# Expert gate and up weights in transfers of 8 MB with 64 KB rows, and a router chain by token tiles

## Chip, cores and metric

The kernel runs on one core of one Trainium2 chip. The metric is the device time of one execution in microseconds. The median of three executions of the kernel before is 1241.34 us (1241.11 to 1243.54).

## What is computed

One decoder layer and a final norm, for one sequence of 256 tokens of width 1024, all in float32:

```
h = x + hybrid_mixer(rms_norm(x))            # gated linear attention beside dilated window attention
h = h + memory_cross_attention(rms_norm(h))  # 4 heads into 256 memory tokens
f = rms_norm(h)
logits = f @ w_router + b_router             # 32 experts
top_logit, top_e = top_k(logits, 4); gate = softmax(top_logit)
h = h + sum over the 4 experts e of gate * ( swiglu(f @ w_gate[e] + b_gate[e], f @ w_up[e] + b_up[e]) @ w_down[e] + b_down[e] )
out = rms_norm(h)
```

`swiglu` is clamped. Every expert is worked through, with up to 64 of its tokens at a time; further rounds follow only if an expert got more than 64.

## The kernel before

The program is written by hand, engine by engine, with semaphores; nothing is reordered by a scheduler. Each of the five engine blocks (`sp`, `pool`, `act`, `dve`, `pe`) runs its own list.

**Dense part.** The mixer's and the cross-attention's weights arrive as 1 MB halves (`HALVES`, `w_dense`) in three raw buffers. ScalarE cuts each half into a float16 high part (line 643) and VectorE into a low part (L969, and for the first half in two pieces, `ahead_cut`, L1020); TensorE multiplies high by high, high by low and low by high (`PASSES`). `feature_major` and `token_major` are the two loops. At the start VectorE and ScalarE square one tile of x each, the normed x is transposed, and `high_T` and `low_T` make its two parts. The results of TensorE go through eight PSUM banks whose use is set by the list `FILLS`: `fill` takes the bank of a name, `take` waits until it is full, `emptied` until it is free again.

**Router.** The output projection of the cross-attention has four blocks, `xo{n}{t}`: column half n, token tile t (128 tokens). VectorE adds each to h (L1289), ScalarE squares it (L657), TensorE transposes h (`residual_T`, L1748), and ScalarE or VectorE copies the transposes to `fT` with the gain `g3` (`routed_T`). After the last block the mean squares of both tiles become roots on GpSimd (`root(6, 8)`, L568), h is split into high and low parts (L890, L1297), the logits of both tiles are scaled (L1313), the top four are found, a matrix product with a triangle gives each token its place (L1789), and two comparisons (L1352) make the selection matrices that the experts' gather needs.

**Experts.** 32 experts in 8 groups of 4 (`EG`), `body` once per group: group 0 written out, 1 to 3 and 4 to 6 in loops, group 7 written out with pieces. Per expert j there are six units of 2 MB, in the order of `ORDER`: gate and up of the first half of the hidden columns, gate and up of the second half, down first half, down second half. Unit v of a group is v = 6j + i. Units go through a ring of `NSLOT` = 8 slots; unit v uses slot `home_index(v)` = (v + 2) mod 8. `unit_left(v - 8)` makes the sync queue wait until TensorE has used up the unit that was in the slot: gate and up units are released by `h_full` at the end of a gate/up pass (L1888), down units by `dn_used` and `y_full` (L1910). The sync queue's loop in groups 1 to 6 is

```
for v in range(0, per, 2):
    unit_left(v - NSLOT, k * EG, z)
    unit_left(v + 1 - NSLOT, k * EG, z)
    load_pair(v, n * EG + v // UPE, z)      # 4 MB: 128 partitions x 32 KB
```

On TensorE an expert is: gate/up pass of the first half (32 matmuls of 512 columns, L1888), transposes (L1901), pass of the second half, transposes, down (32 matmuls, L1910). At expert 0 of a group two gathers (L1829) stand before the first pass and two inside it, after 8 matmuls; the scatter of the expert before (L1839) stands before the group's gathers or between the passes. In group 0 units 10 to 15 are loaded in pieces as the first expert frees its slots (`reused`, `gu_used`). In group 7 the last experts' units come in pieces (`LAST_PIECES`).

**End.** VectorE multiplies the sums by the final gain (`gained`, L1419), ScalarE squares them (L936), VectorE asks for the root (`asked`, L1426), GpSimd takes it, ScalarE and VectorE scale one half each (L940, L1437), and four stores follow.

## Time and profile before

| | |
|---|---|
| median of three executions | 1241.34 us |
| the profiled execution | 1242.41 us |
| its span | 1240.7 us |
| TensorE busy | 1153.2 us (93%), 6687 matmuls |
| VectorE, ScalarE, GpSimd busy | 411.6, 261.6, 20.9 us |
| mean granted TensorE clock | 0.986 |
| moved by the DMA engines | 458.38 MB, 369 GB/s over the span |
| sync queue's share of 16 DMA engines | 87.8% |
| chain that ended last | TensorE 61%, DMA 29%, sync queue 3%, ScalarE 2%, VectorE 2% |

The profiled execution lies 1.07 us above the median. "Busy" counts an engine's instructions, not its waits. The page cuts the span into 40 slices of 31 us: the DMA engines' share is 35 to 85% in the first 11 slices, and 90% or more from the 14th to the last but one, where they move 418 to 435 GB/s. The chain that ended last is followed back from the end, at each step to whatever released it. "DMA ring<-in_w_down" in it is the time from a transfer's issue to its landing.

### The profile page before, as it was taken

To read this page: it belongs to the slowest core of one execution; us is meant where nothing else is said; L and a number is where in the kernel's file an instruction comes from. 1 tells how busy PE (TensorE), PEld (TensorE's weight loads), DVE (VectorE), ACT (ScalarE), POOL (GpSimd) and SP (SyncE) were. 2 spreads that over 40 slices of the span, in tenths; PEclk is the share of its full clock that TensorE was granted. 3 is DMA by queue.
4 is the path that set the end of the run, shared out by engine and by line. 5 is a ranking of instruction groups with operands and counts; after the bars stand their busy time and mean duration, and the time that the engine had idled before them with its cause. 6 is when DMAs were issued, how large, how long until landed. Compare 5 with 4: busy or idle time off the path is not lost.

```text
span 1240.7 us, 16139 instructions
## 1 busy us (share of the span) xinstructions
PE 1153.2 (93%) x6687; PEld 576.8 (46%) x6687; DVE 411.6 (33%) x803; ACT 261.6 (21%) x450; POOL 20.9 (2%) x40
## 2 busy tenths in 40 slices
PE   8999999999999999999989887998998898889887
PEld 7888989887433333333323232432332233224322
DVE  6789474665422222222122112211221122122112
ACT  5655464464400010010001000100110010001001
POOL 4000000000000000000000000000000000000000
PEclk9999999999899999999999999999999999999999
DMA  8455524986699999999999999999999999999996
GB/s 329 173 204 183 190 76 182 382 316 244 239 420 395 430 418 434 429 435 428 435 427 435 430 433 429 431 429 432 431 431 433 431 431 431 435 428 435 419 419 264
DMA packets 30117, 458.38 MB, mean 369 GB/s; under 512 B 3584, under 2 KB 3600, under 8 KB 8816
## 3 DMA queue, kind: packets, MB, share of 16 engines
q1 hardware_dynamic: 28800, 454.57, 87.8%
q0 software_dynamic: 832, 2.51, 0.6%
q8 instruction: 39, 0.64, 0.2%
q10 hardware_dynamic: 432, 0.55, 0.1%
q14 instruction: 14, 0.11, 0.0%
HBM read 456.57 MB, written 1.05 MB: 369 GB/s over the span
## 4 chain that ended last, share of the span: by engine, by line
PE 61%; DMA 29%; SPq 3%; issue 2%; ACT 2%; DVE 2%; POOL 0%; DVEq 0%; ACTq 0%; POOLq 0%
PE bank L1888 22%; DMA ring<-in_w_down 16%; DMA ring<-in_w_gate_up 12%; PE bank L1910 10%; PE bank L1495 4%; PE bank L1472 4%; PE sums L1553 3%; PE sums L1472 3%; SPq L431 3%; PE sums L1839 3%; PE sums L1495 2%; PE bank L1829 2%; PE bank L1553 2%; PE bank L1901 2%; DMA ring<-in_w_dense 1%
## 5 line engine op out<-in xcount | busy, mean ns | idle before, releaser
L1888 PE MATMUL bank<-ring,reg_a 128*64 128x512 f32 x2016 | 457.9, 606 | 42.5 <-DMA ring<-in_w_gate_up 41.8
L1888 PEld LDWEIGHTS bank<-ring,reg_a 128*64 128x64 f32 x2016 | 142.4, 139 | 324.4 <-issue 263.4
L1910 PE MATMUL bank<-ring,reg_ol 128*64 128x512 f32 x1024 | 227.0, 595 | 14.5 <-DMA ring<-in_w_down 12.8
L1389 DVE TENSOR_TENSOR masks<-bank,bT 128x256 f32<-128x256 f32 x64 | 27.2, 424 | 449.7 <-PE bank L1901 449.7
L1910 PEld LDWEIGHTS bank<-ring,reg_ol 128*64 128x64 f32 x1024 | 79.2, 137 | 141.1 <-issue 133.8
L625 ACT ACTIVATE reg_t<-bank 128x512 f32<-128x512 f32 x64 | 38.2, 597 | 440.5 <-PE bank L1888 240.5
L969 DVE SCALAR_TENSOR_TENSOR ring<-ring 128x2048 f16<-128x2048 f32 x47 | 107.3, 2289 | 40.1 <-ACT ring L643 39.8
L643 ACT ACTIVATE ring<-ring 128x2048 f16<-128x2048 f32 x47 | 89.5, 1910 | 32.7 <-PE sums L1553 14.1
L926 ACT ACTIVATE masks<-masks 128x256 f32<-128x256 f32 x64 | 26.7, 417 | 326.4 <-DVE masks L1390 326.4
L1839 PE MATMUL sums<-reg_t,reg_g 64*128 64x512 f32 x256 | 70.1, 634 | 5.5 <-ACT reg_t L625 5.5
L1376 DVE COPY reg_t<-bank 128x512 f32<-128x512 f32 x32 | 22.1, 691 | 159.2 <-PE bank L1888 159.2
L1901 PEld LDWEIGHTS bank<-ident,reg_t 128*128 128x128 f32 x256 | 26.8, 140 | 42.7 <-DVE reg_t L1376 21.8
L1839 PEld LDWEIGHTS sums<-reg_t,reg_g 64*128 64x128 f32 x256 | 20.0, 185 | 55.3 <-issue 42.7
L1901 PE MATMUL bank<-ident,reg_t 128*128 128x128 f32 x256 | 42.0, 287 | 2.5 <-DVE reg_t L1376 1.7
L1553 PE MATMUL sums<-reg_a,ring 128*128 128x256 f16 x384 | 42.3, 273 | 0.0
L1829 PE MATMUL bank<-reg_t,reg_m 128*128 128x256 f16 x256 | 34.0, 291 | 6.5 <-issue 5.8
L1553 PEld LDWEIGHTS sums<-reg_a,ring 128*128 128x128 f16 x384 | 37.5, 98 | 4.6 <-issue 0.3
L1369 DVE TENSOR_TENSOR reg_a<-bank,g 128x512 f32<-128x512 f32 x16 | 11.1, 692 | 80.3 <-PE bank L1829 80.3
L1472 PE MATMUL bank<-reg_a,ring 128*128 128x256 f16 x336 | 37.5, 273 | 0.0
L1829 PEld LDWEIGHTS bank<-reg_t,reg_m 128*128 128x128 f16 x256 | 25.2, 104 | 22.7 <-issue 18.7
L1472 PEld LDWEIGHTS bank<-reg_a,ring 128*128 128x128 f16 x336 | 32.9, 98 | 3.8
L1472 PE MATMUL sums<-reg_a,ring 128*128 128x256 f16 x240 | 27.3, 273 | 1.8 <-DVE reg_a L976 1.8
(323 smaller groups left out, 884.8 us busy)
## 6 DMA issues: line engine op xcount, KB each, us to landing
ring<-in_w_gate_up SPq DMA_DIRECT2D x52, 4096.0 KB, 29.8
ring<-in_w_down SPq DMA_DIRECT2D x26, 4096.0 KB, 30.8
ring<-in_w_dense SPq DMA_DIRECT2D x47, 1024.0 KB, 5.1
ring<-in_w_gate_up SPq DMA_DIRECT2D x10, 2048.0 KB, 9.6
ring<-in_w_gate_up SPq DMA_DIRECT2D x16, 1024.0 KB, 25.5
ring<-in_w_down SPq DMA_DIRECT2D x6, 2048.0 KB, 11.0
ring<-in_w_gate_up SPq DMA_DIRECT2D x16, 512.0 KB, 14.2
ring<-in_w_down SPq DMA_DIRECT2D x12, 512.0 KB, 7.2
```

The lines of the kernel that those rows point to most:

```text
L431: sp.dma_start(home[:, o:o + n], src.rearrange("e p n -> p (e n)")).then_inc(done, 16)
L625: return act.activation(dst, src, ACT.Copy)
L643: act.activation(cut[u % EARLY][:, 0, :], raw[u % EARLY], ACT.Copy, scale=WS).then_inc(w_high, 1)
L969: dve.scalar_tensor_tensor(cut[u % EARLY][:, 1, :], raw[u % EARLY], WS, cut[u % EARLY][:, 0, :], ALU.mult, ALU.subtract).then_inc(w_low, 1)
L1472: ins = mm(b[:, i * T:(i + 1) * T], w[:, pw, c, o:o + P], rhs[:, px, c, :], start=(c == 0 and k == 0), stop=(c == nk - 1 and k == 2))
L1495: ins = mm(b[:, i * n:(i + 1) * n], lhs[:, px, c, t * P:(t + 1) * P], w[:, pw, c, 0:n], start=(c == 0 and k == 0), stop=(c == nk - 1 and k ...
L1553: ins = mm(b[:, i * T:(i + 1) * T], w[:, pw, i, c, :], aT[:, px, c, :], start=(c == 0 and k == 0), stop=(c == C - 1 and k == 2))
L1829: ins = mm(pt[2 + q % 2][:, i * T:(i + 1) * T], f16[:, part, t, 2 * q + i, :], sel[:, t, :], start=(t == 0 and part == 0), stop=(t == TT - ...
L1839: ins = mm(acc[t][nh][:], selT[rows_h, j, t, :], y[rows_h, :], start=False, stop=last and j == EG - 1)
L1888: ins = mm(pt[nh][col:col + 64, :], xg[:, c, j * SLOTS:(j + 1) * SLOTS], loaded(v + i, C, c), start=(c == 0), stop=(c == C - 1))
L1901: ins = pe.transpose(pt[i][:, c * P:(c + 1) * P], hs[:, 4 * i + c, :], ident[:])
L1910: ins = mm(pt[2][64 * nh:64 * nh + 64, :], actT[:, 4 * i + c, :], w[:, nh * 512:(nh + 1) * 512], start=(i == 0 and c == 0), stop=(i == 1 a ...
```

## The change

**8 MB transfers.** `WHOLE` holds the first units of those experts whose four gate and up units lie in four neighbouring slots: v = 0, 6 and 18, that is experts 0, 1 and 3 of a group. In groups 1 to 6 the four units are loaded by two transfers, of partitions 0 to 63 and 64 to 127, each with rows of 64 KB. Both wait for the release of unit v + 3 - 8. TensorE waits for both before it begins the expert.

```diff
+        WHOLE = [UPE * j for j in range(EG) if home_index(UPE * j, None) + 4 <= NSLOT]
...
                 for v in range(0, per - UPE if last else per, 2):
+                    if not last and v in WHOLE:
+                        o = home_index(v, z) * WIDE
+                        whole = A["w_gate_up"][bass.ds(n * EG + v // UPE, 1)]
+                        for half in range(2):
+                            unit_left(v + 3 - NSLOT, k * EG, z)
+                            rows = slice(64 * half, 64 * half + 64)
+                            sp.dma_start(ring[rows, o:o + 4 * WIDE], whole[:, rows].rearrange("e p n -> p (e n)"))\
+                                .then_inc(home_of(v + 2 * half, z, False)[1], 16)
+                        continue
+                    if not last and v - 2 in WHOLE:
+                        continue
...
                         if z is first_round and not first and pieces == 1:
+                            u = v - v % UPE
+                            if not last and v == u and u in WHOLE:
+                                _, other, c2 = home_of(u + 2, z, first)
+                                pe.wait_ge(other, k * (16 * per // NSLOT) + c2)
                             _, done, count = home_of(v - v % 2, z, first)
```

The last expert's first pair is loaded in 4 pieces each in place of 2, and three semaphores are used twice.

The sync queue's loop over a group, before, from v = 0 (a row with `waits` and no DMA is the wait of the DMA under it; `a_h_full` is the release by a gate/up pass, `a_y_full,a_dn_used` that by the down passes):

```order
L422 ISA [waits a_y_full,a_dn_used]
L422 DMA ring<-in_w_gate_up 128x8192
L438 ISA
L422 ISA [waits a_h_full]
L422 DMA ring<-in_w_gate_up 128x8192
L422 ISA [waits a_h_full]
L422 DMA ring<-in_w_down 128x8192
L422 ISA [waits a_y_full,a_dn_used]
L422 DMA ring<-in_w_gate_up 128x8192
```

The same place in the changed program:

```order
L535 ISA [waits a_h_full]
L535 DMA ring<-in_w_gate_up 64x16384
L535 ISA [waits a_h_full]
L535 DMA ring<-in_w_gate_up 64x16384
L429 ISA [waits a_h_full]
L429 DMA ring<-in_w_down 128x8192
L445 REGISTER_ALU
L535 ISA [waits a_h_full]
L535 DMA ring<-in_w_gate_up 64x16384
L535 ISA [waits a_h_full]
L535 DMA ring<-in_w_gate_up 64x16384
```

Experts 0 and 1 now have two 64x16384 transfers each (16384 elements of 4 bytes per row) behind one and the same release of gate/up units; the down pairs and expert 2's pairs stand as before.

**Router by tiles.** The blocks come in the order xo00, xo10, xo01, xo11. The gain `g3` is multiplied into the router weights instead of into the transposed h. Square, root, logits, choice, place and selection are made for tile 0 while TensorE is at xo11, and for tile 1 after it. VectorE's new list (ScalarE's and TensorE's follow it; `ROUTING` sets their banks):

```diff
+            dve.tensor_tensor(w_rt[:], w_rt[:], bc(g3[:], E), ALU.mult).then_inc(consts, 1)
...
+            residual(0, 0)
+            residual(0, 1)
+            mean_square(0)
+            dve.memset(ranked[:, :, 0:TOPK], -FAR)
+            residual(1, 0)
+            routed_T("0b", 4, 4)
+            f_low_part(0, 0)
+            f_low_part(1, 0)
+            chosen(0)
+            residual(1, 1)
+            placed(0)
+            routed_T("1c", 4, 2)
+            mean_square(1)
+            routed_T("1d", 6, 2)
+            emptied(dve, "pos0")
+            selected(0, 0)
+            chosen(1)
+            f_low_part(0, 1)
+            placed(1)
...
+            def awake(n):
+
+                emptied(pe, "rl1")
+                for _ in range(n):
+                    mm(pt[BANK["rl1"]][:], f16[:, 0, 0, 0, :], wide, start=True, stop=True)
```

`awake(2)` stands twice on TensorE: before and after the products that give the places of tile 1 and the totals. It writes to a bank that nobody reads.

TensorE before, from the third output block (bank) to the places:

```order
L1495 MATMUL bank<-ring,reg_t 128x512 x12
L1748 MATMUL bank<-ident,h 128x128 x8
L1495 MATMUL bank<-ring,reg_t 128x512 x12
L1766 MATMUL bank<-reg_a,w_rt 32x256 x4
L1748 MATMUL bank<-ident,h 128x128 x8
L1773 MATMUL bank<-fold,reg_t 128x32 x2
L1778 MATMUL bank<-w_rt,reg_a 128x32 x8
L1785 MATMUL sums<-reg_m 128x512 x4
L1789 MATMUL bank<-route,tri_s 128x64
```

TensorE now, the same stretch:

```order
L1550 MATMUL bank<-ring,reg_t 128x512 x12
L1831 MATMUL bank<-ident,h 128x128 x8
L1550 MATMUL bank<-ring,reg_t 128x512 x6
L1846 MATMUL bank<-reg_a,w_rt 32x128 x8
L1831 MATMUL bank<-ident,h 128x128 x4
L1550 MATMUL bank<-ring,reg_t 128x512 x3
L1837 MATMUL bank<-fold,reg_t 128x32
L1550 MATMUL bank<-ring,reg_t 128x512 x3
L1846 MATMUL bank<-reg_a,w_rt 32x128 x4
L1869 MATMUL bank<-route,tri_s 128x32
L1831 MATMUL bank<-ident,h 128x128 x4
L1876 MATMUL bank<-w_rt,reg_a 128x32 x4
```

The router's matmuls of tile 0 (128 columns), four transposes and the fold now stand inside the last output block, in place of the 256-column ones behind it.

VectorE before, from h's first low part to the selection (`reg_ol` holds the logits and the top eight, `route` the choice and the places, `reg_t` the selection, `reg_m` h's low part):

```order
L1297 SCALAR_TENSOR_TENSOR reg_m<-h,st,reg_m 128x512
L1313 SCALAR_TENSOR_TENSOR reg_ol<-bank,st,b_rt 128x32 x2
L1318 MAX reg_ol<-reg_ol 128x8 x2
L1320 TENSOR_SCALAR st<-reg_ol 128x2
L1321 MEMSET reg_ol 128x2x4
L1323 MATCH_REPLACE reg_ol<-reg_ol 128x36 x2
L1325 TENSOR_TENSOR route<-reg_ol 128x64
L1297 SCALAR_TENSOR_TENSOR reg_m<-h,st,reg_m 128x512
L1328 SCALAR_TENSOR_TENSOR route<-bank,route 128x64
L1330 MEMSET st 128x1
L1331 MEMSET st 128x1
L1352 TENSOR_TENSOR reg_t<-route,iota_s 128x256 x2
```

VectorE now, from tile 1's choice to its selection:

```order
L1347 SCALAR_TENSOR_TENSOR reg_ol<-bank,st,b_rt 128x32
L1350 MAX reg_ol<-reg_ol 128x8
L1351 TENSOR_SCALAR st<-reg_ol 128x1
L1352 MEMSET reg_ol 128x4
L1353 MATCH_REPLACE reg_ol<-reg_ol 128x36
L1354 TENSOR_TENSOR route<-reg_ol 128x32
L1340 SCALAR_TENSOR_TENSOR reg_m<-h,st,reg_m 128x512
L1361 SCALAR_TENSOR_TENSOR route<-bank,route 128x32
L1389 MEMSET st 128x1
L1366 TENSOR_TENSOR reg_t<-route,iota_s 128x256
```

One tile's operations stand where two tiles' stood, and h's low part comes after the choice.

**Start.** The second tile of x is loaded by ScalarE's queue. q_g is multiplied with the highs of all chunks first, then with x's lows, then with the weight's lows, its two halves in two banks (`q_g`, `q_g1`); k_g likewise. VectorE makes all of x's low parts before the second half of the first weight's.

```diff
+            def highs_first(outs, w, cols, before):
+
+                for k, (pw, px) in enumerate(PASSES):
+                    for c in range(C):
+                        before(k, c)
+                        for b, o in zip(outs, cols):
+                            ins = mm(b, w[:, pw, c, o:o + P], aT[:, px, c, :], start=(k == 0 and c == 0),
+                                     stop=(k == 2 and c == C - 1))
...
-            for q in range(2):
+            for q in range(4):
                 low_T("x_T", q, aT, vT[:, 0:8])
             ahead_cut(AHEAD, HALF, w_high, 1, w_low)
-            for q in range(2, 4):
-                low_T("x_T", q, aT, vT[:, 0:8])
```

**End.** In the last group the scatter of expert 30 stands whole before expert 31's gate pass. ScalarE's square of tile 0 no longer waits for VectorE's gain product, and VectorE makes tile 1's product first:

```diff
-            for t in range(TT):
-                dve.wait_ge(acc_full, 2 * t + 1)
-                gained(t, 0)
-            for t in range(TT):
-                asked(t)
+            dve.wait_ge(acc_full, 3)
+            gained(1, 0)
+            asked(0)
+            gained(0, 0)
+            asked(1)
```

## Rows read from the trace of the kernel before

**Rows 1.** Windows: stretch, busy us (count) per engine, TensorE clock, DMA share, GB/s

```profile
250.00:300.00 50.00, 49.37 (x424) 43.52 (x423) 30.93 (x43) 29.83 (x57) 0.70 (x1) 1.00 0.66 250
...
340.00:360.00 20.00, 19.79 (x96) 7.25 (x94) 3.80 (x9) 1.27 (x3) 0.00 (x0) 1.00 1.02 411
...
900.00:1000.00 100.00, 89.14 (x405) 30.81 (x405) 22.96 (x57) 7.18 (x15) 0.00 (x0) 0.98 1.00 431
```

**Rows 2.** Sync queue's waits, whole program: total us, times, longest

```profile
SPq L438 <- PE bank L1888: 483.4, 53, 20.5
```

**Rows 3.** TensorE in order of time, group 1: start, us, line, what, [idle before]

```profile
427.58 2.74 PE L1910 MATMUL bank<-ring,reg_ol 128*64 128x512 f32 x12
...
432.94 1.92 PE L1829 MATMUL bank<-reg_t,reg_m 128*128 128x256 f16 x16
435.01 1.94 PE L1888 MATMUL bank<-ring,reg_a 128*64 128x512 f32 x8
...
438.73 5.37 PE L1888 MATMUL bank<-ring,reg_a 128*64 128x512 f32 x24
...
461.05 7.07 PE L1888 MATMUL bank<-ring,reg_a 128*64 128x512 f32 x32
...
485.27 7.04 PE L1888 MATMUL bank<-ring,reg_a 128*64 128x512 f32 x32
```

**Rows 4.** TensorE in order of time, group 4

```profile
916.97 7.09 PE L1888 MATMUL bank<-ring,reg_a 128*64 128x512 f32 x32 [0.75 <-DMA ring<-in_w_gate_up]
...
926.69 7.09 PE L1888 MATMUL bank<-ring,reg_a 128*64 128x512 f32 x32 [0.98 <-DMA ring<-in_w_gate_up]
...
946.13 8.78 PE L1888 MATMUL bank<-ring,reg_a 128*64 128x512 f32 x32 [2.64 <-DMA ring<-in_w_gate_up]
```

**Rows 5.** Group 0's last two issues, line 431, 393 to 395 us

```profile
L431 SPq DMA_DIRECT2D ring<-in_w_down x2: 328/380/431, 393.7 to 394.1; - x2
...
DMA to landing us min/median/max: 10.0/12.2/14.5
```

**Rows 6.** Sync queue in order of time, group 1's second and fourth gate pair

```profile
413.23 0.34 SPq L422 DMA_DIRECT2D ring<-in_w_gate_up  x1
...
444.33 0.33 SPq L422 DMA_DIRECT2D ring<-in_w_gate_up  x1
```

**Rows 7.** DMA issues with KB and median us to landing; last, line 431 at 315.0

```profile
h<-in_w_gate_up SPq DMA_DIRECT2D x1, 1024.0 KB, 4.7
...
out<-reg_m ACTq DMA_DIRECT2D x2, 256.0 KB, 2.5
...
DMA to landing us min/median/max: 8.3/8.3/8.3
```

**Rows 8.** Windows of 2 us at the first gather and in group 4

```profile
322.00:324.00 2.00, 1.23 (x7) 0.87 (x7) 2.00 (x5) 1.39 (x4) 0.24 (x1) 0.50 0.02 8
...
947.00:949.00 2.00, 2.00 (x6) 0.48 (x4) 0.00 (x0) 0.00 (x0) 0.00 (x0) 0.50 0.95 410
```

**Rows 9.** Window in which 8 KB rows are loaded

```profile
1180.00:1200.00 20.00, 19.40 (x92) 6.61 (x90) 5.08 (x13) 1.43 (x3) 0.00 (x0) 1.00 1.01 422
```

**Rows 10.** Chain of waits from the last output block to the first expert

```profile
316.90 0.71 POOL st L568
...
318.47 0.75 DVE reg_m L1297
...
322.82 3.57 PE bank L1829 x16
326.39 3.06 PE bank L1888 x8
```

**Rows 11.** TensorE in order of time, start

```profile
14.92 9.47 PE L1472 MATMUL sums<-reg_a,ring 128*128 128x256 f16 x84 [1.09 <-DVE reg_a L976]
...
42.14 5.41 PE L1495 MATMUL bank<-ring,reg_a 128*128 128x256 f16 x48 [1.15 <-DVE ring L969]
```

**Rows 12.** All engines in order of time, end

```profile
1233.40 1.02 ACT L936 ACTIVATE reg_g<-sums 128x1024 f32<-128x1024 f32 x1 [2.07 <-PE sums L1839]
```

312 lines of the change are left out of this document (178 added, 134 removed).

## Prediction

> **What bounds the kernel now.** I read the windows by stage first. Up to 300 us the DMA engines move 250 GB/s while TensorE is busy 49.4 of 50 us; from 340 us on they are busy all the time, at 430 GB/s and more, and between 900 and 1000 us TensorE is busy for 89 of 100 us [rows 1]. So the experts' half of the program is bound by the transfers, and TensorE fills in behind them. The sync queue's waits say what the transfers wait for: a ring slot that the gate and up matmuls free, 53 times, 483 us in all [rows 2]. It costs nothing today, as long as enough is queued when the slot comes free.
>
> TensorE's order of time gives the pace of both. In group 1 it isn't held up: expert 1 takes 485.27 - 461.05 = 24.2 us. Expert 0 takes 26.0 us from its first gate matmul (435.01), and 4.7 us of scatter and gather lie between the end of the last down matmuls before it (430.3) and that matmul [rows 3]. A group is 4 x 24.2 + 1.8 + 4.7 = 103.3 us of TensorE. In group 4 its waits end on landings 9.72 us apart (916.97, 926.69, and so on) for 4 MB each [rows 4]: 431.5 GB/s, 12 such per group, 116.6 us. The data is the longer by 13 us a group, and nearly every microsecond in which the DMA engines stand still from 340 us on comes out at the end. That is the yardstick for what follows.
>
> **The change, part by part.** The diff has four parts: the 8 MB transfers, the router's chain, the start and the end. The queue's order shows two 64x16384 transfers where two 128x8192 stood, so it does what it says.
>
> *When the 8 MB are asked for.* Before, each 4 MB pair waited for its own two slots. Now the first byte waits for the fourth slot, unit v+3-8. Of eight slots that leaves four units queued at most, in place of six: the other gate pair and the down pair of the expert before. Where that expert came in 8 MB too, its gate units have all landed when its matmuls begin, and only the 4 MB of down, 9.72 us, are queued when 8 MB more can be asked for. The slot must be free, and the queue's new bytes flowing, within that.
>
> Group 1, first transfer: the last issues of group 0, at 394.11, land 14.5 us later, at 408.6 [rows 5]. Now nothing may be asked for before 413.23, when before the second pair was [rows 6]. A restart costs more than its bytes: 1 MB into an idle queue takes 4.7 us to land where 2.43 would carry it at the steady rate (2.27 over), 2 MB 8.3 where 4.86 would (3.5 over), 256 KB 2.5 for 0.6 (1.9 over) [rows 7]. I take 2.27 after a long gap, 1.9 after a short one; bounds 1.9 and 3.5. Late by 413.23 + 2.27 - 408.6 = **6.9 us**.
> Group 1, expert 1: the release is expert 0's first gate pass, whose last matmul ends at 444.10; the request goes out at 444.33 [rows 3, 6]. The queue would end at 408.6 + 6.9 + 19.4 + 9.7 = 444.6. Late by 444.33 + 1.9 - 444.6 = **1.6**. After that TensorE's lead is gone.
> Groups 2 to 6, expert 0 after expert 3. TensorE has idled before expert 3, so that its first pass runs at half clock for a while: 8.78 us in place of 7.09 after an idle of 2.64 [rows 4], at a granted 0.50, which is 1.2 GHz [rows 8]. From expert 3's landing: 8.8 + 0.2 + 1.9 = 10.9 against 9.7, late by 1.2.
> Groups 2 to 6, expert 1 after expert 0. Expert 0 lands 19.4 + 10.9 = 30.3 us after expert 3. TensorE ends expert 3 at 1.7 + 24.2, scatters and gathers for 4.7 and can begin at 30.6; its first pass with the gathers inside takes 435.01 to 444.10, 9.1 us [rows 3]. 30.6 + 9.1 + 0.2 + 1.9 = 41.8, queue empty at 30.3 + 9.7 = 40.0: late by 1.8.
> Expert 3 after expert 2 (which still comes in pairs) has 38.9 us queued from expert 1's landing, and its release comes at 1.7 + 24.2 + 7.1 = 33: no gap. Group 7 is asked for as before.
> Five groups by (1.2 + 1.8) is **15.0**. Bounds: TensorE warm and 1.9 give 0 + 1.5 a group, 7.5, and with group 1's 6.5 and 2.0 make 16.0; cold and 3.5 give 2.8 + 3.1, 29.5, and with 8.1 and 2.0 make 39.6.
>
> *What longer rows give.* At rows of 8 KB (1180 to 1200 us) the rate is 422 GB/s against 431 to 432 [rows 1, 9]: 4 MB take 9.94 us, 0.22 more, for 24 rows and 3 completions more on each of 16 engines, 8 ns each. A half of 64 rows has 4 rows fewer per engine, 0.033 us; 36 such: **-1.2**. Expert 31's first pair in 4 pieces in place of 2 adds 36 of these, **+0.3**.
>
> *Router.* The fourth output block gets 8 half-width router matmuls, 4 transposes and a fold in its midst: about +1.1 us before TensorE ends it (by the neighbouring matmuls of the same kind). Then only the second tile's chain is left: root, logits, top 4 and places for 128 tokens. Before, the root was taken from 316.90 to 317.61; VectorE then waited until 318.47 for ScalarE's high part and made a low part (0.75) before the logits, and the gather began at 322.82 [rows 10]. Now the low parts of tile 0 are done, tile 1's stands behind its choice, and the two-tile operations are halved: about 2.5 us less. Net **-1.4**, bounds 0 and -3. The first expert's gather (3.57 us) and its first 8 matmuls (3.06) ran at half clock [rows 8, 10]; the four added wide matmuls fill TensorE's pauses. At full clock the same two take 1.92 and 1.94 [rows 3], 2.8 less; I take 6 in 10 of that, **-1.7**. Because the transfers become continuous only when these matmuls free the first units, both count in full. The product of router weight and gain stands where VectorE waits for TensorE anyway: nothing; were it late, 0.4 us.
>
> *Start.* TensorE pauses 1.09 us before 14.92 and 1.15 before 42.14 [rows 11]. Taking all highs first can close the early one, but the one at 42 hangs on VectorE's cuts, which come no earlier, and TensorE would only wait there longer. I take **-0.3**, bounds 0 and -2.2. VectorE's two low parts moved ahead of the weight's second half cost nothing, since the sum before the next cut is the same.
>
> *End.* ScalarE's last square began at 1233.40 behind VectorE's gain product [rows 12]; now it needs only the sums: **-0.7**, bounds 0 and -1. The earlier scatter lies in TensorE's waits: nothing, or 2 us if they were gone.
>
> Sum: 6.9 + 1.6 + 15.0 - 1.2 + 0.3 - 1.4 - 1.7 - 0.3 - 0.7 = **+18.5 us** on the profiled execution's 1242.41, so 1260.9; it lay 1.07 above the median of 1241.34, against which I say **1259.8**. With the bounds: 16.0 of gaps less 9.9 of gains gives 1247; 39.6 of gaps less the rows' 0.9 gives 1280.
>
> **The rivals.** *Faster.* The gaps of groups 2 to 6 do not form, because the next 8 MB are asked for before the down units run out: it decides whether the release comes within about 8 us of the landing, and the warm first pass of 7.09 would make that for expert 0. If the restart also hides, group 1 keeps 413.2 - 408.6 = 4.6. Router, clock and start then give their bounds of 3.0, 2.8 and 2.2, the end 0.7, the rows 0.9: 4.6 - 9.6 = -5.0, 1236.3, and a little less if long rows save more than their count. For it: the front's pauses are in plain sight. Against it: expert 0's first pass takes 9.1 us even warm.
> *Half rate.* A transfer to 64 partitions may reach only half of the paths into SBUF, so that each 4 MB takes 19.4 us and the two halves follow each other: 36 x 9.7 = 349 more than the forecast, 1609. No row shows a large transfer to fewer than 128 partitions, and where all partitions are written a rate per path and a rate per DMA engine look the same, so the trace neither bears this out nor excludes it. It would take a limit at the partitions, where the long queue and the even 9.72 us of every landing [rows 4] fit a limit at the engines just as well: 1 in 10.
> The Trainium skill states such a rule (SBUF — State Buffer, "Door 1: The DMA port swizzle" and "Can I just issue two DMAs to hit both halves?"): partitions 0 to 63 reach 8 of 16 ports, and two transfers to the two halves serialize. It speaks against this change, and by it the time would be this rival's; no run here shows it yet.
> *No change.* The middle of forecast and faster rival, with steady gaps of under 1 us: 1239 to 1244.
>
> **How the numbers follow.** Forecast 0.56, own range 1247 to 1280; faster rival 0.29; no change 0.05; half rate 0.10. A measurement of this kernel tells 0.2% (2.5 us). Faster 0.29, same 0.05, slower 0.66. The range 1235 to 1280 leaves out the half rate and the lower part of the faster rival, under 2 in 10 together.
>
> **What would show it.** Right: DMA share under 1.00 in a window at 408 to 415 us, and twice in each of groups 2 to 6; a request for 8 MB less than 9 us before the landing of the down units; landings of an 8 MB pair 19.4 us after the one before; group periods of about 119.5 us; the first gather at full clock and some 1.5 us earlier. Wrong: periods of 116.6 or less, or of 170 and more, which is the half rate.

## The result, and the profile after

| | before | after |
|---|---|---|
| median, measured together on one chip | 1241.6 us (4 runs, 1241.1 to 1243.5) | 1697.2 us (4 runs, 1695.3 to 1698.1) |
| span of the profiled execution | 1240.7 us | 1695.3 us |
| mean granted TensorE clock | 0.986 | 0.852 |

The change makes the kernel 1.366 times slower (95% interval 1.364 to 1.369), 455.6 us more. The prediction said 1259.8 within 1235 to 1280; it named this outcome as the rival of the half rate, 1609 us, with 1 in 10.

The page of the profile after: busy time, then in 40 slices the share of the DMA engines and what they moved, the chain that ended last, and the costliest group with its idle time.

```profile
PE 1183.3 (70%) x6701; PEld 580.2 (34%) x6701; DVE 411.9 (24%) x807; ACT 261.5 (15%) x451; POOL 21.7 (1%) x41
...
DMA  7454377598999998999999998998999998999997
GB/s 268 172 178 173 125 306 291 227 378 353 199 239 330 279 243 223 223 396 247 206 239 352 267 248 224 260 359 223 209 237 346 272 247 223 260 359 285 433 418 301
...
PE 49%; DMA 48%; DVE 1%; ACT 1%; SPq 1%; issue 1%; ACTq 0%; DVEq 0%
DMA ring<-in_w_gate_up 47%; PE bank L1998 21%; PE bank L2020 6%; PE bank L1550 3%; PE bank L1527 3%; PE sums L1637 2%; PE sums L1550 2%; PE sums L1527 2%; PE sums L1945 2%; PE bank L1935 1%; PE bank L1637 1%; PE bank L2011 1%; DMA ring<-in_w_dense 1%; SPq L535 1%; PE bank L1697 0%
...
L1998 PE MATMUL bank<-ring,reg_a 128*64 128x512 f32 x2016 | 483.8, 634 | 464.0 <-DMA ring<-in_w_gate_up 463.9
```

TensorE does nearly the same work (1183 us busy, 6701 matmuls; before 1153 and 6687) and stands 464 us waiting for gate and up units, where the kernel before has 42. That is almost the whole difference. The two lines to read together are the DMA share and the GB/s under it: in the slices of groups 1 to 6 the engines are as busy as before and move about half as much in many of them. The windows say the same. The first line answers to the last of [rows 1]; of the second, the first 37 us are the landing of one expert's two halves and nothing else:

```profile
900.00:1000.00 100.00, 66.19 (x290) 21.88 (x292) 12.35 (x32) 5.07 (x10) 0.00 (x0) 0.82 1.00 313
...
1000.00:1040.00 40.00, 18.54 (x80) 7.00 (x78) 5.63 (x12) 1.85 (x4) 0.00 (x0) 0.73 0.92 211
```

A share of 1.00 at 313 GB/s and one of 0.92 at 211, where [rows 1] has 1.00 at 431. So most of the missing rate isn't one of idle engines: each of the 16 is occupied and slow. How slow one transfer is shows in the sync queue's issues and how long they took to land (the issue line of the pair asked for at 1049.0 us, then its two landings):

```profile
1049.04 1.14 SPq L535 DMA_DIRECT2D ring<-in_w_gate_up  x2
```
```profile
DMA to landing us min/median/max: 23.6/33.4/43.2
```

The two were issued 0.6 us apart and land 23.6 and 43.2 us after their issues, so 20.2 us apart, where 4 MB to all partitions land every 9.72 us [rows 4]. TensorE's order of time in group 4 answers to [rows 4]:

```profile
904.40 9.36 PE L1998 MATMUL bank<-ring,reg_a 128*64 128x512 f32 x32 [26.64 <-DMA ring<-in_w_gate_up]
984.70 8.47 PE L1998 MATMUL bank<-ring,reg_a 128*64 128x512 f32 x32 [29.41 <-DMA ring<-in_w_gate_up]
```

Waits of 27 to 29 us stand where there were 0.75 to 2.64. A group takes 188 us: expert 3's 8 MB are asked for at 938.15 and again at 1126.34. Before, it took 116.6.

```profile
938.15 1.13 SPq L535 DMA_DIRECT2D ring<-in_w_gate_up  x2
...
1126.34 1.13 SPq L535 DMA_DIRECT2D ring<-in_w_gate_up  x2
```

Some 11 us are lost before the experts begin. TensorE at the start (answers to [rows 11]), and ScalarE beside it:

```profile
22.57 0.84 PE L1615 MATMUL sums<-reg_a,reg_ol 128*32 128x256 f16 x24
35.57 6.88 PE L1550 MATMUL sums<-ring,reg_a 128*128 128x256 f16 x48 [12.16 <-ACT reg_ol L648]
```
```profile
34.47 0.42 ACT L696 ACTIVATE ring<-reg_g 128x256 f32<-128x256 f32 x1 [2.02 <-DVE reg_g L1086]
34.79 1.12 ACT L648 ACTIVATE reg_ol<-sums 128x256 f32<-128x256 f32 x3
```

The new pause of 12.16 us ends with ScalarE's copies of `q_g` and `q_g1` (L648). They stand in ScalarE's list behind the sines of the rotary angles (L696), as the copy of `q_g` always did. But `q_g1` is now in bank 7, which is the bank of `v_g0`, TensorE's next fill.

The router's stretch (answers to the last two of [rows 10]; the first expert's gather is L1935, its first 8 matmuls L1998):

```profile
315.83 5.34 PE L1550 MATMUL sums<-ring,reg_t 128*128 128x512 f16 x24 [1.86 <-issue]
...
336.45 1.91 PE L1935 MATMUL bank<-reg_t,reg_m 128*128 128x256 f16 x16
338.41 1.94 PE L1998 MATMUL bank<-ring,reg_a 128*64 128x512 f32 x8
```

Gather and first matmuls run at full clock, 1.91 and 1.94 us where [rows 10] has 3.57 and 3.06. They begin 13.6 us later, though: 10.6 come from the start, 1.7 from the wait of 1.86 us before the first output matmuls, and 1.4 from the end of the router, where the granted clock is 0.66 (331 to 336 us) although the matmuls that were to keep TensorE busy run there.

### The profile page after: what moved, and what is told of

The parts are those of the page before. It is cut to its first block, busy times and chain, and to the rows that moved or that the text cites. A ratio compares the mean times of both kernels' runs of the same rounds, so it can differ in the third digit from the quotient of the medians.

```text
span 1695.3 us, 16151 instructions
## 1 busy us (share of the span) xinstructions
PE 1183.3 (70%) x6701; PEld 580.2 (34%) x6701; DVE 411.9 (24%) x807; ACT 261.5 (15%) x451; POOL 21.7 (1%) x41
## 4 chain that ended last, share of the span: by engine, by line
PE 49%; DMA 48%; DVE 1%; ACT 1%; SPq 1%; issue 1%; ACTq 0%; DVEq 0%
DMA ring<-in_w_gate_up 47%; PE bank L1998 21%; PE bank L2020 6%; PE bank L1550 3%; PE bank L1527 3%; PE sums L1637 2%; PE sums L1550 2%; PE sums L1527 2%; PE sums L1945 2%; PE bank L1935 1%; PE bank L1637 1%; PE bank L2011 1%; DMA ring<-in_w_dense 1%; SPq L535 1%; PE bank L1697 0%
## 5 line engine op out<-in xcount | busy, mean ns | idle before, releaser
L1998 PE MATMUL bank<-ring,reg_a 128*64 128x512 f32 x2016 | 483.8, 634 | 464.0 <-DMA ring<-in_w_gate_up 463.9
L1998 PEld LDWEIGHTS bank<-ring,reg_a 128*64 128x64 f32 x2016 | 147.5, 145 | 760.9 <-issue 449.8
L645 ACT ACTIVATE reg_t<-bank 128x512 f32<-128x512 f32 (+1 forms) x66 | 38.7, 587 | 755.6 <-PE bank L1998 570.0
L2020 PEld LDWEIGHTS bank<-ring,reg_ol 128*64 128x64 f32 x1024 | 74.1, 137 | 131.9 <-issue 131.9
L1424 DVE TENSOR_TENSOR reg_a<-bank,g 128x512 f32<-128x512 f32 x16 | 11.1, 691 | 220.6 <-PE bank L1935 220.6
L1935 PE MATMUL bank<-reg_t,reg_m 128*128 128x256 f16 x256 | 37.1, 308 | 9.6 <-issue 9.5
L947 ACT ACTIVATE reg_a<-bank,g 128x256 f32<-128x256 f32 x32 | 13.4, 470 | 194.0 <-PE bank L1935 194.0
L1637 PE MATMUL sums<-reg_a,ring 128*128 128x256 f16 x384 | 42.3, 273 | 0.0
L1935 PEld LDWEIGHTS bank<-reg_t,reg_m 128*128 128x128 f16 x256 | 26.9, 110 | 32.4 <-issue 26.7
L1550 PE MATMUL sums<-ring,reg_a 128*128 128x256 f16 x240 | 28.2, 281 | 12.2 <-ACT reg_ol L648 12.2
## 6 DMA issues: line engine op xcount, KB each, us to landing
ring<-in_w_down SPq DMA_DIRECT2D x6, 2048.0 KB, 11.1
```

The lines of the kernel that those rows point to most:

```text
L645: return act.activation(dst, src, ACT.Copy)
L1550: ins = mm(b[:, i * n:(i + 1) * n], lhs[:, px, c, t * P:(t + 1) * P], w[:, pw, c, 0:n], start=(c == 0 and k == 0), stop=(c == nk - 1 and k ...
L1637: ins = mm(b[:, i * T:(i + 1) * T], w[:, pw, i, c, :], aT[:, px, c, :], start=(c == 0 and k == 0), stop=(c == C - 1 and k == 2))
L1935: ins = mm(pt[2 + q % 2][:, i * T:(i + 1) * T], f16[:, part, t, 2 * q + i, :], sel[:, t, :], start=(t == 0 and part == 0), stop=(t == TT - ...
L1998: ins = mm(pt[nh][col:col + 64, :], xg[:, c, j * SLOTS:(j + 1) * SLOTS], loaded(v + i, C, c), start=(c == 0), stop=(c == C - 1))
L2020: ins = mm(pt[2][64 * nh:64 * nh + 64, :], actT[:, 4 * i + c, :], w[:, nh * 512:(nh + 1) * 512], start=(i == 0 and c == 0), stop=(i == 1 a ...
```

## The experiments

Each time stands against runs of the kernel before on the same chip, whose medians were 1242.1 to 1242.2 us. Each edit is against the kernel named with it.

### What in the 8 MB transfers costs

**The transfers alone.** The kernel before, with `WHOLE`, the two transfers of 64 partitions and TensorE's wait for both, and nothing else of the change.

> The kernel before, and of the change the 8 MB transfers alone: two of 64 partitions by 64 KB, and the waits that go with them. Theory A (half rate): each transfer of 4 MB to 64 partitions takes 20.2 us in place of 9.7, 36 of them, so that the time is 1241 + 440 to 450 = 1681 to 1691. Rival B (the prediction: only gaps, because each request waits for the fourth slot): 1241.3 + 6.9 + 1.6 + 15.0 - 1.2 = 1263.6.

1679.98 us, ratio 1.3525 (1.3501 to 1.3550): theory A, within 1.1 us of its range, and far from rival B's 1263.6. The transfers carry 437.8 of the 455.6 us.

**The same bytes and waits, all partitions.** Against the kernel above:

```diff
-rows = slice(64 * half, 64 * half + 64)
-sp.dma_start(ring[rows, o:o + 4 * WIDE], whole[:, rows]...)
+cc = slice(2 * WIDE * half, 2 * WIDE * half + 2 * WIDE)
+sp.dma_start(ring[:, o + cc.start:o + cc.stop], whole[:, :, cc]...)
```

> The kernel before with the requests and waits of the 8 MB transfers, but each of the two transfers goes to all 128 partitions, with rows of 32 KB (half of the columns each). Both theories agree on the waits: gaps of 6.9 + 1.6 in group 1 and 3.0 in each of five more, together 23.5, so 1265 (bounds 16.0 and 39.6: 1257 to 1281). What this run decides is whether the waits take part in the loss: if it takes 1265, the prediction's gaps were right and the other 420 us are of the partitions alone; if it takes 1242 to 1245, gaps do not form at full rate; over 1300 would put the loss on the waits.

1285.74 us, ratio 1.0350 (1.0333 to 1.0367): +43.5 us. So 394.2 of the 437.8 us are of the partitions alone, and the gaps are real but cost nearly twice the forecast of 23.5, somewhat over its upper bound. The sync queue's requests for expert 3, then expert 0, then expert 1 of the next group, and the landings of the middle pair of these (issued at 537.63 and half a microsecond later):

```profile
503.69 0.85 SPq L530 DMA_DIRECT2D ring<-in_w_gate_up  x2
537.63 0.85 SPq L530 DMA_DIRECT2D ring<-in_w_gate_up  x2
569.94 0.85 SPq L530 DMA_DIRECT2D ring<-in_w_gate_up  x2
```
```profile
DMA to landing us min/median/max: 12.0/17.3/22.5
```

The pair lands at 549.6 and 560.6. The down units before it were asked for at 512.39 and landed 25.7 us later, at 538.1. So the request came 0.5 us before the queue ran dry (the forecast's steps give 0.7), and the first transfer is 549.6 - 538.1 - 9.72 = 1.8 us late, where 1.2 was forecast. What was not in the sum is that the second of the pair is late as well: 560.6 - 549.6 = 11.0, 1.3 us over. For expert 1 the down units land at 570.3 and the first transfer 12.3 us after 569.94, at 582.2: 2.2 late where 1.8 was forecast. Together 5.3 us a group in place of 3.0.

Five periods (from one group's request for expert 3 to the next group's) take from 503.69 to 1118.14, 614.5 us, 31.5 more than 5 x 116.6. One of them is longer than the others by 7 to 9 us, from 746.16 to 875.50:

```profile
746.16 0.85 SPq L530 DMA_DIRECT2D ring<-in_w_gate_up  x2
...
875.50 0.85 SPq L530 DMA_DIRECT2D ring<-in_w_gate_up  x2
...
1118.14 0.85 SPq L530 DMA_DIRECT2D ring<-in_w_gate_up  x2
```
```profile
798.17 1.99 PE L1853 MATMUL sums<-reg_t,reg_g 64*128 64x512 f32 x8 [0.70 <-ACT reg_t L639]
805.44 3.55 PE L1843 MATMUL bank<-reg_t,reg_m 128*128 128x256 f16 x16 [5.28 <-issue]
```

There TensorE leaves the loop over groups 1 to 3 and enters the one over 4 to 6: it stands 5.28 us for nothing that the profile shows as a wait, and works at half clock after it (3.55 us for a gather of 1.92). The trace of before has the same pause, 5.77 us up to 775.64; with six units queued it hardly mattered, with four it delays the request to 818.21 us, while the down units asked for at 789.03 landed 24.5 us later, at 813.5: the queue is empty for 4.7 us. The records of the DMA engines hint at what TensorE stands for. In the trace of before, no packet of the queues named "instruction" falls between 540 and 730 us, while the loop turns; between 772 and 776 us, at the end of the pause, there are two (packets, MB, share of the window):

```profile
q8 instruction: 1, 0.02, 1.6%
q14 instruction: 1, 0.01, 0.5%
```

A packet of 16 KB on q8 stands at the end of this pause in all 16 traces. So it is likely that TensorE waits for instructions there; no run tests it.

In group 1 the request goes out at 414.53 (1.3 us later than the forecast's 413.23). Expert 0 then starts at 437.72, on the second landing, and not at TensorE's own 435.01, so that expert 1 is asked for at 447.00 and not at 444.33. Group 1 loses the remaining 12 us, where the sum had 8.5. The landings bear this out. Group 0's last units land at 409.5 and expert 0's first transfer at 426.6, which is 7.4 late; its second lands 11.1 us after that, 1.4 over; the one asked for at 447.00 lands at 460.3, which is 3.2 late, since the down units before it land at 447.4.

**Long rows to all partitions.** Against the kernel above: `cc` is the first 16256 columns in the first transfer, the last 128 in the second.

> As the kernel with the two transfers to all partitions, but the first carries 16256 of the 16384 columns, rows of 65,024 bytes, and the second the last 128. Theory A (the loss is of the 64 partitions): the same time as with rows of 32 KB, within 2 us. Rival C (the loss is of the length of the rows, a packet of 64 KB being slow by itself): these rows are as slow as those of the change, 20 us per 4 MB, 1680 or so.

1287.52 us, ratio 1.0355 (1.0337 to 1.0372): the same as with rows of 32 KB within their intervals, so long rows aren't slow by themselves (theory A). On the 1.2 us that the forecast gave to fewer rows per engine this run says nothing, since its two transfers have 128 rows each, as many as before.

**Even and odd partitions.** Against the transfers alone:

```diff
-rows = slice(64 * half, 64 * half + 64)
+rows = slice(half, P, 2)
```

> The kernel before and the 8 MB transfers with rows of 64 KB to 64 partitions each, but the first takes the even partitions and the second the odd ones, in place of the lower and the upper half. Theory A (each half of the partitions has its own paths into SBUF, and 64 neighbouring rows reach only half of them): the rows of one transfer now lie on all paths, 4 MB take 9.7 us, and the time is that of the two transfers to all partitions. Rival D (a transfer of 64 partitions is slow whichever they are, since it has 4 rows for each engine in place of 8): 1680 as with the halves. Between the two, 1400 to 1600, would say that paths are shared by neighbouring partitions in smaller groups.

1289.88 us, ratio 1.0383 (1.0365 to 1.0401). One slice expression gives back 390 us: theory A. These transfers have 64 rows each, as in the forecast's term of -1.2 for fewer rows, and the kernel is 4.1 us slower than with all partitions, not faster. The windows from 900 to 1000 us of the four kernels in the order above (halves, all partitions, long rows, even and odd) show it in their last two columns:

```profile
900.00:1000.00 100.00, 69.14 (x310) 22.87 (x308) 15.25 (x39) 5.49 (x12) 0.00 (x0) 0.86 0.99 285
```
```profile
900.00:1000.00 100.00, 92.79 (x420) 32.91 (x422) 19.95 (x49) 8.93 (x18) 0.00 (x0) 0.94 0.94 402
```
```profile
900.00:1000.00 100.00, 87.96 (x402) 31.44 (x404) 19.28 (x46) 8.34 (x17) 0.00 (x0) 0.93 0.94 401
```
```profile
900.00:1000.00 100.00, 87.74 (x398) 31.35 (x400) 19.29 (x46) 8.33 (x17) 0.00 (x0) 0.93 0.94 399
```

The slow one has the highest share and the lowest rate; the other three, at a share of 0.94, move 399 to 402 GB/s.

The partition isn't the only thing that differs between halves and even and odd: the source in HBM does too, 4 MB in one piece against every second row of 64 KB. But the down units of an expert are also 4 MB in one piece (128 rows of 32 KB), and so are the rows of the middle 64 partitions in a run further down; both move at the full rate, 9.7 us for the 4 MB.

**Two queues.** Against the transfers alone: expert 0's pair goes to all partitions; for experts 1 and 3 the sync queue issues only the lower half, and ScalarE, when its wait for the same gate pass is over, the upper:

```diff
+if v in WHOLE and z is first_round and not first and not last:
+    act.dma_start(ring[64:, o:o + 4 * WIDE], A["w_gate_up"][...][:, 64:]...).then_inc(..., 16)
```

> The kernel before with 8 MB for the same experts: for the first of a group in two transfers to all 128 partitions; for the other two of a group the lower 64 partitions from the sync queue and the upper 64 from ScalarE's queue, asked for at the same moment, so that both halves can be under way together. Theory A (the limit is at the partitions: half of the paths serve each half): while both transfers are under way all paths are in use, and a pair of 8 MB takes 19.4 us as with all partitions, so the time is near 1286 to 1300. Rival B (an engine that writes 64 neighbouring partitions is slow by itself, whatever else is under way): each 4 MB still costs twice, 24 of them by 10.5: 1286 + 252 = 1540.

1534.15 us, ratio 1.2354 (1.2334 to 1.2374), rival B's number. But the records show that this run doesn't speak for rival B's reason against theory A's: the two halves were hardly ever written at the same time. The DMA records that begin in 700 to 704 us and in 705 to 709 us, by queue (q1 is the sync queue's, q10 ScalarE's):

```profile
q1 hardware_dynamic: 15, 0.98, 115.5%
q10 hardware_dynamic: 1, 0.07, 7.7%
```
```profile
q10 hardware_dynamic: 15, 0.98, 115.5%
q1 hardware_dynamic: 1, 0.07, 7.7%
```

Each stretch has 16 packets of 64 KB, one for each engine. In the first, 15 engines take a lower row; in the second, 15 take an upper one. A packet takes 115.5% of 16 x 4 us / 15 = 4.9 us, where 64 KB at the full rate take 2.43 (9.72 / 4). Each engine takes turns between its two queues, and all began together, so that the 16 stand on one half of the partitions at a time and then all on the other. That is half rate by theory A too. Rival B falls with the next run. Whether engines out of step would reach the full rate was not tried.

**The middle 64 partitions, then 32 and 32.** Against the transfers alone:

```diff
+for rows in (slice(32, 96),) if half == 0 else (slice(0, 32), slice(96, 128)):
+    done = sides if rows.start == 0 else home_of(v + 2 * half, z, False)[1]
```

(The lower 32 are issued second and the upper 32 third; TensorE waits for all three.)

> The kernel before and the 8 MB for the same experts with rows of 64 KB, in three transfers: the middle 64 partitions (32 to 95), then the upper 32, then the lower 32, asked for together once the fourth slot is free. Theory A1 (each half of the partitions has half of the paths, shared by all its partitions): the middle 4 MB lie half and half and take 9.7 us, the two 2 MB pieces at half rate 9.7 each, 29.1 us per 8 MB in place of 19.4, and the time is 1286 + 18 x 9.7 = 1461. Theory A2 (a path belongs to a few neighbouring partitions, so that only the number of different partitions counts): the middle 64 are as slow as the lower 64, 20.2 us, and 32 partitions reach a quarter of the paths, 2 MB in 20.2 us each; 60.6 us per 8 MB, 1286 + 18 x 41.2 = 2028. Theory D (an engine that writes rows of fewer than 8 neighbours is slow by itself, whichever they are): as the halves, 20.2 + 10.1 + 10.1 = 40.4 us per 8 MB, 1664.

1495.09 us, ratio 1.2039 (1.2019 to 1.2059). The issue line of one triple, its landings after each issue, and the landing of the down units asked for before it, at 669.31:

```profile
684.81 1.69 SPq L532 DMA_DIRECT2D ring<-in_w_gate_up  x3
```
```profile
DMA to landing us min/median/max: 15.0/24.2/33.5
```
```profile
DMA to landing us min/median/max: 20.4/20.4/20.4
```

The down units land at 689.7 and the middle 4 MB 10.1 us later, at 699.8: full rate, within 4%. The two pieces of 2 MB to 32 partitions follow at intervals of 9.9 and 10.0 us, where 4.86 is the full rate: half rate. This is A1: 64 partitions half below and half above 64 are as fast as 128, 32 on one side as fast per byte as the 64 of that side. A2 and D had the middle transfer at 20.2 us. Rival B of the run before, by which an engine that writes 64 neighbouring partitions is slow by itself, falls too, since the middle 64 are neighbours. The time is 34 us over A1's 1461; five periods (527.48 to 1316.26) take 157.8 us each, 34.9 more than with all partitions, of which 3 x (30.0 - 19.4) = 32 are the slower transfers; the rest are longer gaps.

**Do the parts add?** The changed kernel with the even and odd slices of above.

> The changed kernel, whole, with the one edit that its two transfers take the even and the odd partitions in place of the lower and the upper half. If the partitions alone carry the loss above the gaps, the two parts add: 1289.9 with even and odd in the kernel before, and 13.2 for router, start and end: 1303 (1300 to 1306), some 394 us under the changed kernel. Over 1320 would say that the parts make each other worse.

1305.15 us, ratio 1.0506 (1.0488 to 1.0523). They add, within 2.2 us: 47.7 for the transfers with their gaps, 13.2 for the rest, 63.1 measured.

### The rest of the change

**Without the 8 MB transfers.** The changed kernel with `WHOLE = []`.

> The changed kernel with the gate and up units again in 4 MB transfers to 128 partitions (the list of whole experts is empty); router, start and end stay as changed. Theory A (from the trace after): the 8 MB transfers cost some 445 us and the rest of the change costs 11: the start is 10.6 late (TensorE's new stall of 12.2 us), router and clock together 0.3, the pieces 0.3, the end -0.1. Time 1252.4, between 1250 and 1255; from 340 us on the DMA engines run at 430 GB/s again. Rival B (the prediction's own terms for these parts: router -1.4, clock -1.7, start -0.3, end -0.7, pieces +0.3): 1237.5. A time over 1300 would say that the loss isn't in the 8 MB transfers.

1255.3 us, ratio 1.0106 (1.0092 to 1.0121): +13.2 us. Router, start and end together make the kernel slower, as theory A has it (1250 to 1255). In this execution the first gather ran mostly at half clock (3.11 us, answering to the 1.91 of the kernel after; granted 0.50 from 334 to 337 us, 0.59 to 340), so the clock isn't safe in this order:

```profile
337.04 3.11 PE L1935 MATMUL bank<-reg_t,reg_m 128*128 128x256 f16 x16
340.08 1.94 PE L1998 MATMUL bank<-ring,reg_a 128*64 128x512 f32 x8
```

**The copy of `q_g1` early.** Against the kernel above:

```diff
+unscaled(qg[:, 1, :], take(act, "q_g1")[:, 0:T]).then_inc(free_bank("q_g1"), 1)
 cut_ahead("v_g0")
...
-unscaled(dst[:, 1, :], take(act, "q_g1")[:, 0:T]).then_inc(free_bank("q_g1"), 1)
```

> As the kernel with the 4 MB transfers, but ScalarE copies the second half of the queries' low-rank product out of bank 7 just before it cuts the next weight, and so ahead of the rotary angles. Theory A: TensorE's stall of 12.2 us is there only because the next fill of bank 7 waits for this copy; with the copy at about 23 us the stall goes and 10 us or more come back: 1241 to 1242.5. Rival B: the stall is one of the cut weights of that fill, which come late anyway (the weight's second half lands at 24.6 in place of 19.1): half of it or less comes back, 1247 or more.

1247.28 us, ratio 1.0046 (1.0034 to 1.0059): 8.0 us come back, and the time is rival B's (1247 or more), though it is more than half of the stall. The stall of 12.2 is gone, so A is right about its cause; B is right that the cut weights come late anyway: two smaller pauses stand behind it, where [rows 11] has one of 1.15 us:

```profile
37.23 5.41 PE L1550 MATMUL bank<-ring,reg_a 128*128 128x256 f16 x48 [2.36 <-DVE ring L1006]
44.40 5.41 PE L1550 MATMUL bank<-ring,reg_a 128*128 128x256 f16 x48 [1.75 <-DVE ring L1006]
```

**The gain product one operation earlier.** Against the kernel above, on VectorE `w_rt * g3` stands ahead of `out_low("xpv0")`.

> As the kernel with the early copy, and the product of router weight and gain stands one operation earlier in VectorE's list, ahead of the low part of the last attention output. Theory A: the first output matmul waited for that product (1.9 us before 315.8 in the trace after, where 0.4 us was normal); 1.3 us come back, 1.0 to 1.5 less than the kernel with the early copy. Rival B: the low part that now stands behind the product is itself what the first output matmuls wait for, so that nothing changes, within 0.3 us.

1244.57 us, ratio 1.0023 (1.0014 to 1.0031): 2.7 us less. The first output matmuls now begin 1.8 us after the attention's last ones (302.96, then 304.76), as before the change (301.39, then 303.19), where the kernel above had 3.83; the third output block begins 7.35 us after them in place of 9.01. That explains 1.7 of the 2.7. Another 1.4 lie in the router's last matmuls, which ran at a granted 0.57 in the profiled execution of the kernel above (323 to 327 us) and at 1.00 in this one; whether that goes with the product or differs from run to run is open, since the changed kernel with even and odd partitions has the late product and a clock of 1.00 there.

**One place of keeping busy less.** Against the kernel above, without the first `awake(2)`.

> As the kernel before it, without the first of the two places where TensorE runs two matmuls only to stay busy (ahead of the places of tile 1). Theory A: the choice is ready 1.2 us before TensorE gets to it, because of these matmuls, so 0.8 us come back and the first gather stays at full clock. Rival B: without them the granted clock falls to 0.5 before the gather, which then takes 3.6 us in place of 1.9 and the first 8 matmuls 3.1 in place of 1.9: 2 us more, not less.

1245.14 us, ratio 1.0025 (1.0010 to 1.0040): no difference from the kernel above that could be told, since seven runs lie between 1241.5 and 1247.5. In the profiled execution the gather stayed at full clock (1.91 us), against B; A's 0.8 us don't show either.

**VectorE's cut ahead of the last two low parts.** Against the kernel with the gain product earlier, the start's order on VectorE as before the change:

```diff
-for q in range(4):
+for q in range(2):
     low_T("x_T", q, aT, vT[:, 0:8])
 ahead_cut(AHEAD, HALF, w_high, 1, w_low)
+for q in range(2, 4):
+    low_T("x_T", q, aT, vT[:, 0:8])
```

> The kernel with the 4 MB transfers, the early copy and the earlier gain product, with one thing more undone: VectorE cuts the low half of the first weight before the last two low parts of x, as before the change. Theory A: that cut frees the slot for the next weight's transfer; with it 1.6 us later (15.72 against 14.11 us) the transfer queued behind the small tables and landed 5 us later, and TensorE got two pauses of 2.4 and 1.8 us at 36 and 44 us in place of one of 1.15. Undone, the request is back at 14.1 us and 1.5 to 2.5 us come back: 1242 to 1243. Rival B: the order of x's two loads on two queues is what delays the weights, and nothing changes: 1244.6.

1241.40 us, ratio 0.9994 (0.9985 to 1.0003): 3.2 us less than with the cut late, theory A and somewhat more than its 1.5 to 2.5. The sync queue asks for the next weight half at 14.06 us in place of 15.56, and of the two pauses one is left, beside a short one of 0.43 us:

```profile
42.20 5.42 PE L1551 MATMUL bank<-ring,reg_a 128*128 128x256 f16 x48 [1.75 <-DVE ring L1006]
```

**The whole start undone.** The 4 MB transfers, the earlier gain product, the start as before; router and end as changed.

> The kernel with the 4 MB transfers and the earlier gain product, and the start (loads of x, the order of the first matmuls, ScalarE's and VectorE's first operations) as it was before; of the change the router's chain by token tiles and the end are left. Theory A: in the kernel with the early copy and this product the attention's last matmuls still came 1.6 us later than before (302.96 against 301.39 us) and the first 8 expert matmuls ended 1.2 us earlier (328.27 against 329.45); with the start undone the whole 2.8 us show: 1242.06 - 2.8 = 1239.3, and this version beats both kernels. Rival B: what the front wins is not passed on to the end, because the transfers are paced by something else: 1242, no change.

1242.14 us, ratio 0.9999 (0.9990 to 1.0009). The front does what theory A says: the first 8 expert matmuls end at 326.45, 3.0 us before the 329.45 of [rows 10]. In the kernel before, the first output matmuls stood at 303.19 (second fence).

```profile
302.95 1.46 PE L1545 MATMUL sums<-ring,reg_t 128*128 128x512 f16 x6
...
322.55 1.91 PE L1901 MATMUL bank<-reg_t,reg_m 128*128 128x256 f16 x16
324.51 1.94 PE L1964 MATMUL bank<-ring,reg_a 128*64 128x512 f32 x8
```
```profile
303.19 1.46 PE L1495 MATMUL sums<-ring,reg_t 128*128 128x512 f16 x6
```

The time doesn't move: rival B. Its profiled execution has a span of 1239.1, 1.6 us under before's 1240.7, but over 11 runs nothing is left. The two traces show where part of the 3 us goes. The sync queue's requests for gate and up units, in this kernel and then in the kernel before:

```profile
506.86 7.19 SPq L428 DMA_DIRECT2D ring<-in_w_gate_up  x2
...
532.82 0.33 SPq L428 DMA_DIRECT2D ring<-in_w_gate_up  x1
```
```profile
509.86 7.19 SPq L422 DMA_DIRECT2D ring<-in_w_gate_up  x2
...
534.26 0.33 SPq L422 DMA_DIRECT2D ring<-in_w_gate_up  x1
```

The lead is 3.0 us as long as TensorE sets the pace, 1.4 from the time on when it waits for landings (its first such wait here is at 515.70), and 1.6 at the last stores. So the 3 us of TensorE are only about half of that in the transfers. Why the medians don't show even this isn't settled. No version found beats both kernels by more than can be measured.

**Neither place of keeping busy.** Against the kernel above.

> As the kernel before it, without either of the two places where TensorE runs wide matmuls only to stay busy. Theory A (they keep the granted clock at 1.00 over the first gather and the first 8 expert matmuls): the gather takes 3.1 to 3.6 us in place of 1.9 and the 8 matmuls 3.1 in place of 1.9, against 0.6 to 1.2 us saved: 1.5 to 2 us slower than the kernel with them. Rival B (the clock is up because the router's chain leaves fewer pauses): the same clock, 0.6 to 1.2 us faster.

1242.63 us, ratio 0.9997 (0.9987 to 1.0006): the same; B's 0.6 to 1.2 us don't show. The clock stays up without them in the profiled execution (B's reason, granted 1.00 from 318 to 326 us), so in this order the matmuls added for it do nothing that shows:

```profile
322.15 1.91 PE L1899 MATMUL bank<-reg_t,reg_m 128*128 128x256 f16 x16 [0.52 <-ACT reg_ol L931]
324.12 1.94 PE L1962 MATMUL bank<-ring,reg_a 128*64 128x512 f32 x8
```

## Why the prediction was wrong

**The step that failed** is the choice between the forecast and the rival of the half rate. The prediction said that even landings "fit a limit at the engines just as well" and gave a limit at the partitions 1 in 10. What the runs showed in its place: the partitions below 64 take half of the full rate together (4 MB in 20.2 us for 9.72), and so do those from 64 up; which partitions on a side didn't matter, for the sets tried. The lower 64 and the upper 64, and 32 on one side, run at half rate. All 128, the even 64, the odd 64 and the middle 64 run at full rate. A transfer to one half keeps all 16 engines occupied, each at half speed (4.9 us for a packet of 64 KB in place of 2.43), and this is why the share of busy DMA engines says nothing of it.

The Trainium skill (SBUF — State Buffer, "Door 1: The DMA port swizzle") says that bit 6 of the partition number picks the side and that 0 to 63 reach no more ports than 0 to 31; the transfers of halves, of the middle 64 and of 32 agree. Its section "Can I just issue two DMAs to hit both halves?" says that two such transfers serialize, and that issuing from several engines doesn't help; the run with two queues agrees that nothing is gained, though packet by packet its two transfers alternate. It says further that only one transfer spanning all 128 partitions reaches all ports; here the middle 64 alone took 10.1 us for 4 MB, so the measurement decides against that sentence. The prediction had this rule of the Trainium skill, and the trace had no row that spoke against it: absent such a row, a rule stated for exactly this shape should have weighed far more than 1 in 10.

**The rival's price** was 36 x 9.7 = 349 on top of the forecast. Measured are 20.2 us for 9.72, so 36 x 10.5 = 377, and 394.2 between halves and all partitions. The other 17 were not taken apart; they lie most likely in the gaps, since TensorE idles before these experts and starts them at a lower clock (8.5 to 9.4 us for a pass of 7.09, granted 0.73 to 0.82 in the windows after).

**Gaps, group 1**: 6.9 + 1.6 forecast, about 12 measured at full rate. The step "the release is expert 0's first gate pass, whose last matmul ends at 444.10" took TensorE's time from before (a start at 435.01), though it now has to wait for both transfers, until 437.7. And here too the second transfer is late as well, by 1.4 us.

**Gaps, groups 2 to 6**: 15.0 forecast, 31.5 measured. Place and cause were right, twice a group: this part of the forecast's mechanism came as told, and only its size was off. The term for the restart was undersized (the second transfer after a gap is late too, by 1.3 us), 5.3 a group in place of 3.0; and TensorE's 5 us between the two loops was left out, though it stood in the trace before.

**Longer rows**, -1.2 for fewer rows per engine: not seen; with 64 rows of 64 KB on even and odd partitions the kernel is 4.1 us slower than with 128 of 32 KB. Where these 4.1 us lie is open.

**Router**, -1.4: nothing. From the first output matmul to the gather it is 19.63 us before (303.19 to the 322.82 of [rows 10]) and 19.60 in the kernel with the start undone (302.95 to 322.55). The halved operations save what the added ones cost. In the changed kernel as it stands it is 20.6 (315.83 to 336.45), with the clock at 0.66 near the end.

**Clock**, -1.7: the full 2.8 us came in the trace after and in all the kernels with the changed router but one. The number came, but the reason given, the added wide matmuls, isn't borne out: without them the clock is the same, and with them it fell once before the gather (0.66 in the trace after) and once within it. That the term's sign was right is luck.

**Gain product**, "nothing; were it late, 0.4 us": it was late, and 1.7 us, because the first output matmuls wait behind it and not only the router.

**Start**, -0.3: +10.6 us to the start of the experts. Two steps failed. The prediction followed TensorE's new order but not the bank of the new fill, whose release stands behind the sines on ScalarE (8 us of the median). And "VectorE's two low parts moved ahead ... cost nothing" counted VectorE's sum alone: the cut that moved back frees the slot for the next weight, whose request is 1.6 us later (3.2 us of the median).

**End**, -0.7: -0.1. From the last sums' matmuls to the last store's issue it is 5.84 us (1686.14 to 1691.98) after and 5.93 before: ScalarE's first square begins 0.8 us earlier, and then its second waits for VectorE's product.

**The yardstick**, that a microsecond before the experts counts in full: not borne out for 3 us, by the kernel with the start undone; larger losses came through (10.6 + 1.7 + 1.4 - 2.8 = 10.9 to the end of the first 8 expert matmuls in the trace after, 12.6 in that of the kernel with 4 MB transfers, and 13.2 in its median).

The parts of the 455.6 us: 394.2 half rate, 43.5 gaps, 13.2 start and router, and 4.7 that appear only when all stand together (2.2 of them also with even and odd partitions).

## What to carry to other kernels

Ask of each DMA which side of partition 64 its rows lie on, and give every large transfer equally many on both. The mark of one that doesn't was, here, a share of busy engines near 1.00 with few GB/s beside it. When a fill gets a bank of its own, look where in the reader's list the release of that bank stands, and when an operation is moved, which slot or buffer it frees and who asks for it. Before a queue is made shallower, look for the longest pause of the engine that frees its slots anywhere in the trace, hidden ones included.

## What was unexpected of the hardware

- Issued from two queues at one moment, two transfers were served packet by packet in turn on each engine, and nearly all 16 engines turned together: 15 of 16 packets from one queue, then 15 of 16 from the other.
- Two transfers of 4 MB to 64 partitions land 20.2 us apart, 4% worse than half of the full rate (2 x 9.72).
- After the queue has run dry or nearly so, the first 4 MB to all partitions were 1.8 to 3.2 us late, and a second transfer right behind was late too in two of four places, by 1.3 and 1.4 us.
- Between two loops of the program TensorE stands 5.1 to 6.5 us in most traces, and 9.5 to 10.2 in three with half-rate transfers (the changed kernel, the transfers alone, the middle 64). The profile shows no wait there, but a 16 KB packet of an instruction queue stands at the pause's end.
